# A fourth seven-product pair in each gated feed-forward layer, on the same eight weight buffers

## The reference

```python
def swiglu(x, w_in, w_out):
    gate, up = jnp.split(x @ w_in, 2, axis=-1)
    return (jax.nn.silu(gate) * up) @ w_out
...
h = layer_norm(DN_ALPHA * h + 0.5 * swiglu(h, ffn_w_in[i, 0], ffn_w_out[i, 0]), ...)
```

## Time and profile before

| | us |
|---|---|
| median of 3 runs | 1490.11 (1489.75 to 1490.24) |
| profiled execution | 1489.8 |
| its span, first to last instruction | 1487.8 |
| PE busy | 1478.4 (99% of the span) |
| VectorE busy | 1114.9 (75%) |
| ScalarE busy | 833.9 (56%) |
| granted clock, mean | 0.998 |

### The profile page before, as it was taken

The page is one execution under the profiler, slowest core; times in us unless marked ns, Lnnn a source line. Parts: engine busy times, 40 slices in busy tenths (PEclk is TensorE's granted clock), DMA queues, the critical chain, the costliest instruction groups (busy, mean ns, idle before and its releaser), DMA issues.

```text
span 1487.8 us, 18609 instructions
## 1 busy us (share of the span) xinstructions
PE 1478.4 (99%) x7654; PEld 1256.3 (84%) x7654; DVE 1114.9 (75%) x1135; ACT 833.9 (56%) x839; POOL 150.4 (10%) x152
## 2 busy tenths in 40 slices
PE   9999999999999999999999999999999999999997
PEld 8888888888888888888888888888998888888886
DVE  7899777778978789686576878967785566776565
ACT  6665566656656567454434656746555666454343
POOL 0102010200002000033030200002002200020000
PEclk9999999999999999999999999999999999999999
DMA  9886554597658676655445677665444344465551
GB/s 394 237 284 206 212 199 174 217 332 239 178 190 311 227 244 179 251 206 201 170 142 184 274 248 245 179 242 194 163 170 171 142 142 170 145 242 180 198 198 57
DMA packets 46595, 310.08 MB, mean 208 GB/s; under 512 B 5568, under 2 KB 6016, under 8 KB 10800
## 3 DMA queue, kind: packets, MB, share of 16 engines
q1 hardware_dynamic: 38592, 270.35, 48.3%
q0 software_dynamic: 6112, 34.80, 10.7%
q10 hardware_dynamic: 1808, 3.74, 0.7%
HBM read 282.60 MB, written 1.05 MB: 191 GB/s over the span
## 4 chain that ended last, share of the span: by engine, by line
PE 99%; DVE 0%; issue 0%; ACT 0%; POOLq 0%; POOL 0%; DVEq 0%
PE psum L2011 17%; PE psum L2015 16%; PE psum L2014 16%; PE psum L2120 9%; PE psum L2147 6%; PE psum L2261 5%; PE psum L2257 5%; PE psum L2258 5%; PE psum L2124 5%; PE psum L2154 3%; PE psum L2043 2%; PE psum L2056 2%; PE psum L2049 2%; PE psum L2023 1%; PE psum L2338 1%; PE psum L2278 1%
## 5 line engine op out<-in xcount | busy, mean ns | idle before, releaser
L1189 DVE TENSOR_TENSOR weights_lo<-weights_raw,weights_hi 128x2048 fp32r<-128x2048 f32 x187 | 430.9, 2308 | 219.5 <-ACT weights_hi L613 218.0
L613 ACT ACTIVATE weights_hi<-weights_raw 128x2048 fp32r<-128x2048 f32 x194 | 364.2, 1882 | 194.0 <-PE psum L2015 136.2
L2011 PE MATMUL psum<-weights_hi,hidden_hi 128*128 128x512 f32 x448 | 175.7, 392 | 0.4 <-DVE weights_lo L1189 0.4
L2014 PE MATMUL psum<-weights_lo,hidden_hi 128*128 128x512 f32 x448 | 174.9, 390 | 0.0
L2015 PE MATMUL psum<-weights_hi,hidden_lo 128*128 128x512 f32 x448 | 174.4, 389 | 0.0
L2011 PE MATMUL psum<-weights_hi,operand 128*128 128x512 f32 x384 | 151.5, 394 | 0.0
L2014 PE MATMUL psum<-weights_lo,operand 128*128 128x512 f32 x384 | 149.8, 390 | 0.0
L2015 PE MATMUL psum<-weights_hi,operand 128*128 128x512 f32 x352 | 137.2, 390 | 0.0
L1189 DVE TENSOR_TENSOR weights_lo<-weights_raw_more,weights_hi 128x2048 fp32r<-128x2048 f32 x52 | 119.6, 2300 | 0.8 <-ACT weights_hi L613 0.8
L2120 PE MATMUL psum<-operand,weights_hi 128*128 128x512 f32 x480 | 114.3, 390 | 0.0
L613 ACT ACTIVATE weights_hi<-weights_raw_more 128x2048 fp32r<-128x2048 f32 x52 | 99.5, 1915 | 8.2 <-DVE weights_raw_more L1385 7.7
(11 more groups left out here) (402 smaller groups left out, 2864.6 us busy)
## 6 DMA issues: line engine op xcount, KB each, us to landing
weights_raw<-in_weights SPq DMA_DIRECT2D x194, 1024.0 KB, 4.8
weights_raw_more<-in_weights SPq DMA_DIRECT2D x52, 1024.0 KB, 8.7
weights_raw_more<-weights_raw_more POOLq DMA_DIRECT2D x8, 1024.0 KB, 8.6
normalised<-in_weights SPq DMA_DIRECT2D x8, 1024.0 KB, 9.4
weights_raw_more<-weights_raw POOLq DMA_DIRECT2D x8, 1024.0 KB, 6.9
ln_rows<-in_ln_rows POOLq DMA_DIRECT2D x16, 512.0 KB, 8.5
weights_raw<-normalised POOLq DMA_DIRECT2D x4, 1024.0 KB, 13.1
weights_raw<-weights_raw_more POOLq DMA_DIRECT2D x4, 1024.0 KB, 13.1
```

The lines of the kernel that those rows point to most:

```text
L613: nc.scalar.activation(hi[:, rest], whole[:, rest], ACT.Copy).then_inc(hi_split, 1)
L1189: nc.vector.tensor_tensor(lo_of(n), raw_of(n), hi_of(n).bitcast(F32), ALU.subtract).then_inc(lo_split, 1)
L2011: mm(out, a_hi, b_hi, start=start, stop=False, skip_group_check=True)
L2014: mm(out, a_hi, b_lo, start=False, stop=False, skip_group_check=True)
```

## The change

`GROUPS` becomes (3, 5, 7, 9): steps 3 and 10, plain before, are made in pairs too, so that a layer has four pairs, three plain steps (0 to 2) and 45 operands. What else changes:

- The last pair (9 and 10) ends in the layer's last product. Its rows are transposed in two parts, one for each block of 128 tokens (`turn_last`, `last_hidden_hi`, `last_hidden_lo`), the first inside down 7, the second inside `block_product`; down 8 is no longer in the pair. `last_step` goes.
- The loads of the last pair's up tiles and of down 7 may use raw slots 3 to 7 alone (`in_last`).
- The first down tile of each pair is loaded only when the pair's t1 has been added (`HELD`), in SyncE's queue.
- At the head of a layer the split of down 0 comes ahead of the forms on ScalarE, and ahead of the hidden tile's low part of step 1 on VectorE; two of the forms' low parts move behind the sums of step 2; in layers 1 to 3 the split of the first t1 comes ahead of the sums of step 2.

```diff
-GROUPS = (4, 6, 8)
+GROUPS = (3,5,7,9)
...
-SUMMED = FFN_STEPS - 2 - 2 * len(GROUPS)
+SUMMED = FFN_STEPS - 1 - 2 * len(GROUPS)
...
-WIDE_FROM, WIDE_TO = RING, UP_AT[FFN_STEPS - 1]
+WIDE_FROM, WIDE_TO = RING, FFN_TILES - 3
...
+            in_last += [w and k >= FFN_LOADS.index(("up", GROUPS[-1], 0)) for k, w in enumerate(inside)]
...
         allowed = range(RAW_SLOTS if in_xn[m] else XN_SLOT if wide_load[m] is not None else RING)
+        if in_last[m]:
+            allowed = range(RING, RAW_SLOTS)
...
+for f, n0 in enumerate(FFN_STARTS):
+    for k, s in enumerate(GROUPS):
+        HELD[LOAD_OF[n0] + FFN_LOADS.index(("down", s - 2))] = 16 * (len(GROUPS) * f + k + 1)
...
+                if m in HELD:
+                    sp.wait_ge(t1_added, HELD[m])
...
+                def last_hidden_hi(s, tb):
+
+                    act.wait_ge(group_turned, 2 * group_index(f, s) + tb + 1)
+                    rows = slice(tb * P, (tb + 1) * P)
+                    nc.scalar.activation(hid_hi[:, 0:4, rows], turned_rows(tb), ACT.Copy).then_inc(hid_hi_done, 1)
...
-                    if j == 2 and after in GROUPS:
+                    if j == 2 and after in GROUPS and not f:
                         second_of_next(after, n0 + GROUP_AT[after] + 1)
...
                     split_hi(n + 8)
-                    if s != GROUPS[-1]:
-                        split_hi(n + 9)
+                    if s == GROUPS[-1]:
+                        act.wait_ge(weights_used, n + 7)
+                        last_hidden_hi(s, 0)
+                    split_hi(n + 9)
                     act.wait_ge(weights_used, n + 8)
                     nc.scalar.activation(gate_up[:, 0, :], work[:, 0, 0:TOK], ACT.Silu).then_inc(group_silu, 1)
+                    if s == GROUPS[-1]:
+                        split_hi(n + 10)
+                        last_hidden_hi(s, 1)
...
                 hidden_hi(j0, 0, two(acc[:, 3, :]))
+                split_hi(n0 + 6)
                 forms_hi()
...
-                        if after in GROUPS and j > 2:
+                        if after in GROUPS and (f or j > 2):
                             second_of_next(after, ahead + 1)
...
+                    if f and j == 2 and after in GROUPS:
+                        split_lo(n0 + GROUP_AT[after] + 1)
...
+                    if j == 2:
+                        forms_lo(range(2, 4))
...
+                    if last:
+                        first_rows.then_inc(hid_done, 1)
+                        split_lo(n + 7)
                     split_lo(n + 8)
                     dve.wait_ge(group_silu, 3 * g + 2)
                     nc.vector.tensor_tensor(hid[:, 3, :], gate_up[:, 1, :], p5[:, up], ALU.mult)
-                    if s != GROUPS[-1]:
-                        split_lo(n + 9)
+                    if last:
+                        last_hidden_lo(0)
+                    split_lo(n + 9)
                     dve.wait_ge(group_silu, 3 * g + 3)
...
+                def turn_last(g, s, tb):
+
+                    pe.wait_ge(hid_done, j0 + s + 1 + tb)
...
-                    next_down(s - 2, n + 6)
+                    last = s == GROUPS[-1]
+                    next_down(s - 2, n + 6, {(1, 0, 1): lambda: turn_last(g, s, 0)} if last else {})
                     pe.wait_ge(combined, 3 * g + 3)
                     product(n + 7, 0, block_of_x(1, 1), False)
-                    next_down(s - 1, n + 8, {(1, 0, 1): lambda: turn_group(g, s)})
+                    if not last:
+                        next_down(s - 1, n + 8, {(1, 0, 1): lambda: turn_group(g, s)})
...
-                block_product(n0 + FFN_TILES - 3, hid_ready, lambda tb, s: j0 + FFN_STEPS - 2 + s, hidden_chunks((2, 0, 1), 2),
-                              final=(1, 3, 4, 6)[f])
+                last_group = group_index(f, GROUPS[-1])
+                block_product(n0 + FFN_TILES - 3, hid_ready, lambda tb, s: j0 + FFN_STEPS - 2 + (tb + 1 if s else 0),
+                              hidden_chunks((2, 0, 1), 2), final=(1, 3, 4, 6)[f],
+                              hooks={(0, 1, 0, 0): lambda: turn_last(last_group, GROUPS[-1], 1)})
```

More of the change, by code:

```diff
@@ L373, in build @@
         by_chunk = lambda t: t.rearrange("p (c t) -> p c t", c=4)
+        turned_rows = lambda tb: work[:, 2:4, :].rearrange("p k (c t) -> p (k c) t", c=2)[:, :, tb * P:(tb + 1) * P]
         p1, p6 = squares[:, 0:NCOL], squares[:, NCOL:2 * NCOL]
@@ L401, in build @@
         sig_of = lambda half, b: sig[3 if (half, b) == (1, 2) else b]
-        wide = ["ffn0", "gla2", "gla3", "ffn1", "ffn2", "ret1", "ret2", "ret3", "ret4", "ffn3", "sec1", "sec2", "sec8", "sec9"]
+        wide = ["gla2", "gla3", "ret1", "ret2", "ret3", "ret4", "sec1", "sec2", "sec8", "sec9"]
         half_value = lambda what: wide.index(what) + 1
-        copies_of = lambda what: 1 if what.startswith("ffn") else 2
-        copied_value = lambda what, half: sum(copies_of(w) for w in wide[:wide.index(what)]) + half + 1
+        copied_value = lambda what, half: 2 * wide.index(what) + half + 1
         ret_count = lambda u: 6 + u // 2
@@ L764, in ffn @@
                         group(j, n0 + GROUP_AT[j])
[L765 to L771, removed]
+                        second_of_next(after, ahead + 1)
+                        group_hidden_hi(j)
                         if after in GROUPS:
@@ L1317, in hidden_lo, with last_hidden_lo @@
                                             ALU.subtract).then_inc(hid_ready, 1)
[L1319 to L1328, removed]
+                def last_hidden_lo(tb):
+                    dve.wait_ge(hid_hi_done, j0 + FFN_STEPS - 1 + tb)
+                    rows = slice(tb * P, (tb + 1) * P)
+                    nc.vector.tensor_tensor(hid_lo[:, 0:4, rows], turned_rows(tb), hid_hi[:, 0:4, rows].bitcast(F32),
+                                            ALU.subtract).then_inc(hid_ready, 1)
                 def form_sums():
@@ L1343, in form_sums, with forms_lo @@
                                                    op1=ALU.subtract).then_inc(form_summed, 4)
-                def forms_lo():
-                    for k in range(4):
+                def forms_lo(which):
+                    for k in which:
                         dve.wait_ge(form_hi_done, 4 * f + k + 1)
@@ L1366, in summed_step @@
                                                 ALU.add).then_inc(up_summed if at else gate_summed, 1)
+                    if j == 2:
+                        forms_lo(range(2, 4))
                     if after in GROUPS:
-                        if j == 2:
+                        if not f and j == 2:
                             split_lo(n0 + GROUP_AT[after] + 1)
@@ L1428, in ffn @@
                 summed_step(1, 2)
-                forms_lo()
+                forms_lo(range(2))
                 units = ffn_units()
@@ L1434, in ffn @@
                         group(j, n0 + GROUP_AT[j])
[L1435 to L1441 removed]
+                        split_lo(ahead + 1)
+                        group_hidden_lo(j)
                         if after in GROUPS:
@@ L1446, in ffn @@
                         ahead = n0 + UP_AT[j] + 3
-                        split_lo(ahead - 1)
+                        if j > 2:
+                            split_lo(ahead - 1)
                         split_lo(ahead)
@@ L2280, in turn_group @@
                             ins.then_inc(group_turned, 1)
+                def turn_last(g, s, tb):
+                    pe.wait_ge(hid_done, j0 + s + 1 + tb)
+                    src = hid[:, :, :].rearrange("p c t -> p (c t)")
+                    for c in range(4):
+                        at = (c % 2) * TOK + tb * P
+                        ins = nc.tensor.transpose(work[:, 2 + c // 2, at:at + P], src[:, tb * NCOL + c * P:tb * NCOL + (c + 1) * P], ident)
+                    ins.then_inc(group_turned, 1)
                 def group(s, n, pairs_free):
```

48 lines of the change are left out of this document (20 added, 28 removed).

## The result

The changed kernel takes 1495.86 us (median of 6 runs, 1494.61 to 1496.62) against 1490.19 of the kernel before on the same chip (6 runs): a ratio of 1.0037, 95% interval 1.0027 to 1.0048. It is 5.7 us slower, where 2 us faster was forecast. The profiled execution is the longest of the six, 1496.62, with a span of 1494.8.

What follows compares the result with a forecast made beforehand. The prediction took TensorE (PE), with work in 99% of the span, to bound the kernel: 1489.8 - 10.0 + 1.5 + 6.0 + 0.4 = 1487.7, with the median 0.3 above: 1488.0 us. The range was 1481.5 to 1495.

Steps and rivals of the forecast that it cites:

- PE's saving: Every layer: plain steps 3 and 10 go, a pair comes; 27.89 out, 25.37 in, 2.5 us a layer, 10.0 in all.
- the late tile: Last pair: (up, 10, 0) gets slot 7, released only in the pair before; lands at 417.6, sum issued at 418.1.
- VectorE's chain: In a pair, VectorE's gapless work beginning with first sum t1; starting x late stops PE for x - 1.2 us.
- landing less 10.1: Last pair: the t1 sum may land 10.1 us after its issue; landing later stops PE.
- the landing, 10.4 to 12 us: Last pair: the t1 sum, issued at 418.1, lands at 428.5 to 430.1, 0.3 to 1.9 late.
- 1.5 a layer, 6.0 in all: Last pair of each layer: PE's stop because the t1 sum lands late; bounds 0 and 4.3 a layer.
- one more at 421.9: Last pair: a further tile's load requested at 421.9, after the one at 417.94 within 0.2 us of the sum.
- Both stretches that the prediction set against each other: Load and sum take turns from 45 to 49 (72% and 32%); load alone has 94% from 485 to 489.
- waits for the load and shares with the one after it: Rival, last pairs' sum: 13.4 us to landing, 3.3 a layer, 13.2 in all, 1495.2 us; chance 0.22.
- its two rows: That rival's evidence: earlier sums of 37.50 and 483.95, needing 14.4 and 12.4 us, each with a load within 0.2 us.
- Layer 0's first pair: First pair, layer 0: sum lands at 41.3 behind queued loads, stopping PE for 1.5 us; bounds 0 and 4.9.
- The end of the layer: Behind the last pair's seventh product, VectorE owes PE the second token block; 0.1 a layer, 0.4 charged.

Runs made afterwards that it cites:

- with the tile early: Changed kernel with one line of the slot table altered so that (up, 10, 0) may use any slot and takes slot 1: 1481.92 us, ratio 0.9943.
- the run with one load: Changed kernel, its last pair's wait on t1 in SyncE's queue moved ahead of (up, 10, 1), so only (up, 9, 1) loads beside the sum: 1489.94 us.
- with the load behind the sum: Changed kernel, (up, 9, 1) requested on GpSimd's signal behind the last pair's t1 sum: 1496.76 us; with a small write before the signal: 1481.87 us.
- without the wait on SyncE: Changed kernel with the wait on t1 in SyncE's queue left out everywhere: 1497.73 us, ratio 1.0050.
- the run with the load well behind: Changed kernel, (up, 9, 1) requested on GpSimd's signal, given after the t1 sum's instruction and a small write: 1481.87 us, ratio 0.9944.

## Why the prediction was wrong

**Right: PE's saving.** 2.5 us a layer were forecast; layers without stops are 2.5 shorter (142.87 and 142.91 before, 140.39 and 140.43 with the tile early). The 10.0 are there and were paid back.

**Right: the place and the limit.** The prediction found the late tile, its slot, the sum, and VectorE's chain. Its formula, landing less 10.1, gives 3.8, 2.9 and 2.9 us for layers 1 to 3 with the measured landings of 13.9, 13.0 and 13.0; the layers lost 3.9, 2.9 and 2.9 (differences of the table plus 2.5). What it did not foresee is that the lateness shows at three places, two products and the down tile: PE catches up with VectorE's chain three times. And in layer 0 the limit is tighter (below).

**Wrong: the landing, 10.4 to 12 us; it was 13.0 to 14.3.** This is the term "1.5 a layer, 6.0 in all". The step that failed is the second load: "one more at 421.9" was named and then not charged. For one load the forecast was nearly right: in the run with one load the four sums land after 11.2, 12.8, 11.6 and 11.6 us, 11.8 in the mean, against 11.6 (10.1 and the 1.5). With the second load beside it they need 14.3, 13.9, 13.0 and 13.0. The shares of the queues in layer 1 (packets, MB, share of the engines; q1 loads, q0 sums), 406 to 410 and 413 to 416 us, show both:

```profile
q1 hardware_dynamic: 103, 0.84, 93.0%
...
q0 software_dynamic: 51, 0.42, 66.7%
q1 hardware_dynamic: 45, 0.37, 30.4%
```

First the load (up, 9, 1), queued 0.17 us ahead, has the engines and the sum nothing; later the sum shares with (up, 10, 1), queued behind it. Both stretches that the prediction set against each other are true, one after the other, and the rival "waits for the load and shares with the one after it" is what happened: 13.4 us and 1495.2 were its numbers, 13.0 to 14.3 and 1495.86 the measured ones. It had 0.22. That its total fits to 0.7 us is in part luck: it charged 1.4 too much for the first pair and the end, and missed the 1.7 of layer 0 (below). The evidence against it was that its two rows had other causes too; but both had a load within 0.2 us of the sum, and no other row did.

One reading is that of a load and a sum the one queued first is moved first. The two runs with the load behind the sum bear it out: requested 0.07 us behind the start of the sum's instruction of 0.84 us, the load goes first (sum 14.4 us); requested 1.1 us behind it, the sum does (8.8 us). But it does not cover all stretches. The load (up, 10, 1), requested 3.8 us behind the sum, shares with it. And without the wait on SyncE, two loads requested 5.8 and 0.4 us ahead of layer 0's first sum share with it too, and land 1.5 us ahead of it and 1.6 behind it; the queues of that run from 36 to 42 us:

```profile
q0 software_dynamic: 109, 0.88, 70.0%
q1 hardware_dynamic: 111, 0.78, 32.4%
```

So it is shown that in the last pair 1 us in the order of request decides; what makes a load and a sum go one by one or share is open. The turn-by-turn rule of the Trainium skill (DMA: Bandwidth & Descriptors, Queues, rings and completion order) agrees with the second stretch and with this one, not with the first. The Trainium skill also says (Perfetto Trace Analysis, DMA Instruction — SWDGE (GPSIMD)) that what a profile shows as such a transfer's instruction on GpSimd is the making of its descriptors. That fits the two runs with the load behind the sum, where the first request fell inside those 0.84 us and the second after them. It stays an inference from landings; no trace shows a queue's content.

**Wrong and small.** Layer 0's first pair stopped for 0.5 us by PE's steps, 1.5 charged. The sum was issued at 30.2; the loads ahead of it had 100% of the engines from 30 to 32, and from 33 to 37 the sum had them nearly alone. The prediction counted from the last landing, 34.4, but a load's bytes are over before it lands, and the sum landed at 39.2 in place of 41.3. What the stop of 0.5 hangs on is then no longer the sum: ScalarE takes t1 up at 40.67, behind a copy for step 2, and with the prediction's own chain behind that VectorE is done at 61.6; PE starts the down tile at 61.79. The queues in these two stretches:

```profile
q1 hardware_dynamic: 119, 0.84, 99.9%
...
q0 software_dynamic: 105, 0.86, 103.2%
q1 hardware_dynamic: 7, 0.04, 2.4%
```

The end of the layer has its margin: nothing was lost there, 0.4 charged; only in the run with one load did PE wait once, at the hook inside down 7 (0.8). The wait on SyncE was charged at 0 and is worth 2 to 3 us.

Three slips in the working changed none of this: the terms of the layer's end add up to 27.3, not 27.5; four stops outweigh the other terms from a landing of 12.1 us on (10.1 + 8.1 / 4), while 12.8 or 12.9 is where the kernel would be slower by 3 us; and five loads of 4.8 would make 24 us, more than the 22 that they were said to fit.

**Missed: VectorE's slower splits in layer 0.** Layer 0 lost 5.9 (3.40 and 2.5), and by the formula its last pair should have lost 4.2 (14.3 - 10.1). Two of VectorE's splits in this pair take 3.13 us in place of 2.29, while GpSimd scales the residual:

```profile
150.23 5.46 POOL L550 TENSOR_SCALAR residual<-residual 128x1024 f32<-128x1024 f32 x2
151.64 3.13 DVE L1197 TENSOR_TENSOR weights_lo<-weights_raw_more,weights_hi 128x2048 fp32r<-128x2048 f32 x1
154.69 3.13 DVE L1197 TENSOR_TENSOR weights_lo_more<-weights_raw_more,weights_hi_more 128x2048 fp32r<-128x2048 f32 x1
```

That makes VectorE's chain 1.7 longer here and the limit 8.4 us. From the start of its first product to that of its seventh a last pair without stops takes 22.2 us (414.72 to 436.96 in layer 1 with the tile early), this one 28.1 (138.06 to 166.19): 5.9 lost, which is 4.2 + 1.7. With the same 1.7 the formula gives 2.8 for layer 0 of the run with one load and 1.5 for that of the run with the load well behind; by the same measure 2.8 and 1.65 were lost. The two slow splits stand in every run, in the kernel before at 130.82 and 133.88 (3.13 each), ahead of the one wait in the layers, of 0.4, that the prediction took for small. (Layer 0 had been 0.6 longer than the others before the change, so the 0.5 of its first pair does not come on top of the 5.9.) That GpSimd's work is what slows the two splits is argued from the overlap alone: no run moves it, and beside other work of GpSimd most splits keep 2.29.

The granted clock also fell there, and this cost nothing. Windows of the changed kernel (length; busy PE, PEld, DVE, ACT, POOL; clock; DMA):

```profile
145.00:147.40 2.40, 0.50 (x4) 0.08 (x2) 2.40 (x3) 2.25 (x2) 0.00 (x0) 1.00 1.03 434
147.40:151.00 3.60, 3.60 (x9) 2.82 (x10) 3.60 (x2) 2.43 (x3) 3.24 (x5) 0.53 1.03 312
```

Behind the first stop, 1.9 us, the granted clock was 0.53 for 3.6 us, about the 1.2 GHz level; PE's work in them would have taken 1.7 us less at the full clock (3.6 x 0.47). But PE had to wait for VectorE anyway: in the run without the wait on SyncE the clock stayed at 1.00, and PE stopped for 1.73 at the next late product, where the changed kernel shows no wait. PE's stops in layer 0's last pair, the changed kernel first, then that run:

```profile
147.37 1.92 PE L2277 MATMUL psum<-weights_lo,operand 128*128 128x512 f32 x4 [1.90 <-DVE weights_lo L1197]
160.17 0.47 PE L2027 MATMUL psum<-weights_hi,hidden_hi 128*128 128x512 f32 x1 [1.10 <-DVE weights_lo L1197]
...
149.38 1.20 PE L2275 MATMUL psum<-weights_lo,operand 128*128 128x512 f32 x4 [1.85 <-DVE weights_lo L1195]
156.84 1.19 PE L2275 MATMUL psum<-weights_lo,hidden_hi 128*128 128x512 f32 x4 [1.73 <-DVE weights_lo L1195]
162.19 0.47 PE L2025 MATMUL psum<-weights_hi,hidden_hi 128*128 128x512 f32 x1 [1.08 <-DVE weights_lo L1195]
```

From the beginning of the first stop to the down tile it is 14.7 us in both (145.47 to 160.17, and 147.53 to 162.19), with sums of 14.3 and 14.2; the run with the load behind the sum, its clock at 1.00 as well, has 14.7 too (144.96 to 159.65).

So: 10.0 saved; 15.6 lost (5.9, 3.9, 2.9, 2.9) where 7.9 were charged.

## What to carry to other kernels

When a transfer is on the critical path, look at what is queued just ahead of it, not only at how full the engines are: a load of 4.8 us by itself, requested 0.1 us earlier, took a sum of 6.9 us to 11.2 to 12.8, and a second load to 13.0 to 14.3. Moving the request by 1 us, or the tile to a slot that is free earlier, cost nothing here. And where a trace shows two behaviours of a shared resource, ask what differed in their order of arrival before choosing a value between them; charge every neighbour that you have named. Before a stretch at a low clock is charged, see whether the engine would have waited in it anyway.

## What was not expected of the hardware

- A load requested 0.07 us after the sum's instruction had started still went first (sum 14.4 us); one requested 1.1 us after it did not (8.8 us).
- Two of VectorE's splits of a whole tile take 3.13 us in place of 2.29 in layer 0, where GpSimd scales the residual beside them; a split beside the start of four of GpSimd's transfers keeps 2.28 (147.24 in the changed kernel).
- The granted clock fell behind a stop of 1.9 us in layer 0 of the changed kernel, and did not in the run without the wait on SyncE, behind one of the same length (1.85 us) at the same place in the layer. Windows of that run:

```profile
147.00:149.40 2.40, 0.55 (x4) 0.12 (x2) 2.40 (x3) 2.24 (x2) 0.00 (x0) 1.00 0.33 140
149.40:153.00 3.60, 3.60 (x16) 2.99 (x17) 3.60 (x2) 2.45 (x3) 3.23 (x5) 1.00 0.63 125
```

What set the two apart these runs do not show.
